# Building the expert gates: three bf16 parts against one fp32 product per token, with the scaling on ScalarE

## The chip, the cores and the metric

The kernel runs on one core of a Trainium2 chip, as one launch. The metric is the device time of that launch in microseconds (us). Five engines work side by side and meet only at semaphores: TensorE (PE, matrix products; PEld is its weight load), VectorE (DVE), ScalarE (ACT), GpSimd (POOL) and SyncE (SP), which here issues most of the DMAs.

## The reference, cut to what matters

Two trunk layers of a hybrid model are applied to 128 context ("prompt") tokens and 256 latent ("sample") tokens of width 1024. The change lies in the last part of each layer, a product-key expert mixer. Each token picks 16 experts for each of 8 heads, so 128 of 128 x 128 = 16384 experts, each with a gate from a softmax; an expert's number is i1 x 128 + i2.

```
e_idx = take_along_axis(cand_i, pos)          # 128 experts per token
gate  = softmax(top_s)                        # 8 heads x 16
a     = gelu(einsum('tkd,td->tk', peer_u[e_idx], x)) * gate
out   = einsum('tk,tkd->td', a, peer_v[e_idx])
```

## The kernel before, in words

The 128 prompt tokens are handled sparsely. Their expert rows (u and v, 8 KB each pair) are gathered from HBM, one expert of every token at a time (128 "rows" m per layer): POOL issues the gather, DVE takes the dot product with u (`dot_row`, line 1519), ACT applies Gelu and multiplies with the gate (`coefficient(m)`, lines 972 and 974), and DVE adds coefficient times v (`add_row(m)`, line 1513). `prompt_row` is `add_row(m)` followed by `dot_row` for m+1.

The 256 sample tokens are handled densely. TensorE computes the scores of all 16384 experts, 128 experts ("a panel") at a time, for all 256 tokens (`scores_u`, lines 512 to 517; a panel is split into a high and a low part, `split_panel_hi` on ACT, line 382, `split_panel_lo` on DVE or POOL, line 387). Each score panel goes through Gelu on ACT (line 965) into `act_t`, is multiplied there by the gate of each (token, expert), which is zero for most, and is multiplied with the v panels (`outputs_v`, line 704).

The dense gate table is built on TensorE, in two chunks of 64 values of i1. For a batch of 8 tokens, and for each token t of it, the gates are the product of two small matrices over that token's 128 choices: one-hot rows of i2 (128 x 128, tile `hot2`) and one-hot rows of i1 times the gate (128 x 64, tile `hot1`). The gate is fp32; it is cut into three bf16 parts (`gate_t`), so that each token takes three accumulating bf16 products (line 696). There are 32 batches per chunk.

Order of work in a layer around the change: first 64 score panels (with the routing of the tokens on DVE beside them). Then the **gating stage**, one batch and one score panel by turns, 32 times: on PE `scores_u`, then `build_gates(0, ...)`. Then a stage of scores and v panels ("mixed"). Then the **plain stage**, 32 times `outputs_v` followed by `build_gates(1, ...)`, with one prompt row per batch. Then the other v panels alone.

The order on each engine is the program's order. In the gating stage DVE does for batch w: `one_hots(w)`, `gate_acts(w-1)` (line 1584, the product's result times `act_t`), in every fourth batch (u = 0) a `prompt_row`, and in odd batches a `split_panel_lo`; ACT does `split_panel_hi` for two panels ahead and Gelu, with a `coefficient` first in every fourth batch; POOL does the `split_panel_lo` of even batches. In the plain stage DVE does `one_hots(w)`, `gate_acts(w-1)`, `prompt_row(w)`, and ACT only one `coefficient` per batch. `one_hots(w)` waits until the product of batch w-2 is done (two buffers); the product of batch w waits for `hot1`, `hot2` and for `gate_acts(w-2)`.

Of `one_hots`, four instructions per batch on DVE: `eq1` and `hot2` by comparing (line 1561), and two multiplications of `eq1` with the three gate parts into `hot1` (line 1569). The four tokens of a side lie interleaved in these tiles.

Of the kernel before, what the change touches and what calls it, by code (L numbers as in the profile page):

```python
# [27 lines left out]
BF16 = mybir.dt.bfloat16  # L28
U32 = mybir.dt.uint32
ALU = mybir.AluOpType  # L30
ACT = mybir.ActivationFunctionType
# [3 lines left out]
P = 128  # L35
# [17 lines left out]
HK = PH * TOPK  # L53
# [14 lines left out]
SLOTS = 4  # L68
# [15 lines left out]
TD = TS  # L84
DENSE = TD // P
CHUNKS = 2
CHUNK = NK // CHUNKS
BATCH = 8
SIDE = 4
NB = TD // BATCH  # L90
PARTS = 3
HALF = NB
SEATS = CHUNK + HALF
EARLY_G, HALF_G = CHUNK // SLOTS, HALF // SLOTS
# [3 lines left out]
RING = SLOTS  # L98
# [4 lines left out]
PLAIN_ROWS = MIXED_ROWS + HALF  # L103
LAST_ROWS = PLAIN_ROWS + HALF
# [15 lines left out]
def build(nc, panels, mod_panels, rows, x_in, c_in, vecs, g_final, k_cache, v_cache, bias_in, mask_in, dft_in,  # L120
# [4 lines left out]
    def place(name, where, cols, dt=F32):  # L125

        size = 2 if dt == BF16 else 4
        return nc.alloc_sbuf_tensor_at(name, [P, cols], dt, offset=where), where + size * cols


    raw, o = place("raw", base, SLOTS * D)
    split_hi, o = place("split_hi", o, 2 * D, F32R)
    split_lo, o = place("split_lo", o, 2 * D, F32R)
    h_hi_at = o
    h_hi, o = place("h_hi", o, KT * T, F32R)
    h_lo_at = o
    h_lo, o = place("h_lo", o, KT * T, F32R)
    x, o = place("x", o, KT * T)
    ident, o = place("ident", o, P)
    iota, o = place("iota", o, P)  # L140
    ones, o = place("ones", o, P)
    mask, o = place("mask", o, GRID_W)
    vec, o = place("vec", o, DEPTH * VEC)
    modv, o = place("modv", o, N_MOD * KT * 2)
    gain, o = place("gain", o, 2 * KT * 2)
    gfin, o = place("gfin", o, KT)
    softm, o = place("softm", o, 2 * 16)
# [4 lines left out]
    qkvf, o = place("qkvf", arena, 4 * KT * T)  # L152
    q, k, v, f = (qkvf[:, i * KT * T:(i + 1) * KT * T] for i in range(4))
    gate01, o = place("gate01", o, 2 * KT * T)
# [3 lines left out]
    conv, o = place("conv", o, KT * PAD)  # L158
    u_hi, o = place("u_hi", o, KT * T, F32R)
    u_lo, o = place("u_lo", o, KT * T, F32R)  # L160
    bias, o = place("bias", o, 2 * 2 * TS)
    kc_at = o
    kc, o = place("kc", o, HEADS * CTX)
    vc, o = place("vc", o, HEADS * DH)
    prob_at = o
    prob, o = place("prob", o, 2 * SCORES)
    prob_t, o = place("prob_t", o, 2 * SCORES)
    dft, o = place("dft", o, DFT)
    silu_c, mixer_end = place("silu_c", o, 2 * D)

    cc_s, o = place("cc_s", prob_at, 2 * T)
    ccx, o = place("ccx", o, 2 * PAD)
    cb_s, o = place("cb_s", o, 2 * T)
# [4 lines left out]
    f_hi, o = place("f_hi", arena, KT * T, F32R)  # L178
    f_lo, o = place("f_lo", o, KT * T, F32R)
    fy, _ = place("fy", o, 2 * TT * 512)  # L180

    sq, o = place("sq", arena + 4 * TT * D, KT * T)
    hf, o = place("hf", o, KT * T)
    ms, o = place("ms", o, T)
    rstd, _ = place("rstd", o, T)

    act_t, o = place("act_t", arena, SEATS * TD)
    late_seats = arena + 4 * CHUNK * TD
    act_end = o
    rowbuf, o = place("rowbuf", o, RING * ROW)  # L190
    htmp, _ = place("htmp", o - 4 * ROW, D)
    eq, eq_end = place("eq", o, 2 * HK * TOPK, BF16)
    hot2, o = place("hot2", o, 2 * BATCH * P, BF16)
    eq1, o = place("eq1", o, 2 * BATCH * CHUNK, BF16)
    hot1, o = place("hot1", o, 2 * BATCH * PARTS * CHUNK, BF16)
    assert eq_end <= o
    route_t, o = place("route_t", o, 2 * TD, BF16)
    gate_t, o = place("gate_t", o, PARTS * TD, BF16)
    gate_f, o = place("gate_f", o, TD)
    rest, o = place("rest", o, TD)  # L200
    index, o = place("index", o, SIDE * P, BF16)
    dots, o = place("dots", o, HK)
    dots_g, o = place("dots_g", o, HK)
    coef, o = place("coef", o, HK)
    gate0_r, o = place("gate0_r", o, HK)
    row_at, o = place("row_at", o, HK, U32)
    zeros, o = place("zeros", o, 2 * TD, BF16)
# [9 lines left out]
    sc2, o = place("sc2", o, TT * NK)  # L217
# [133 lines left out]
    def col(t, n, width=T):  # L351
        return t[:, n * width:(n + 1) * width]
# [147 lines left out]
    def _(pe):  # L500
# [44 lines left out]
        with pe.Fori(0, DEPTH) as l:  # L545
# [139 lines left out]
            def build_gates(chunk, turn, u):  # L685

                batch = (l * CHUNKS + chunk) * NB + turn * SLOTS + u
                pe.wait_ge(acts_gated, batch + 1)
                pe.wait_ge(hot2_ready, batch + 1)
                pe.wait_ge(hot1_ready[u % 2], (l * CHUNKS + chunk) * (NB // 2) + turn * 2 + u // 2 + 1)  # L690
                for t in range(BATCH):
                    seat_of = lambda h: h.rearrange("p (g j t) -> p g t j", g=BATCH // SIDE, t=SIDE)[:, t // SIDE, t % SIDE, :]
                    w = seat_of(col(hot2, u % 2, BATCH * P))
                    parts = col(hot1, u % 2, BATCH * PARTS * CHUNK)
                    for c in range(PARTS):
                        last = mm(col(bank[2 + u % 2], t, CHUNK), w, seat_of(col(parts, c, BATCH * CHUNK)), start=(c == 0),  # L696
                                  stop=(c == PARTS - 1))
                last.then_inc(gate_mm, 1)

            def outputs_v(act_at, g, s, last=False):  # L700
# [67 lines left out]
    def _(act):  # L768
# [42 lines left out]
        with act.Fori(0, DEPTH) as l:  # L811
# [182 lines left out]
            for t in range(DENSE):  # L994
                act.wait_ge(route_tr, l * DENSE + t + 1)
                copy(route_t[:, :].rearrange("p (j t) -> p j t", j=2)[:, :, t * P:(t + 1) * P],
                     bank[4 + t][:, 0:2 * P].rearrange("p (j t) -> p j t", j=2))
                copy(col(gate_t, t, P), col(bank[4 + t], 2, P))
                copy(col(gate_f, t, P), col(bank[4 + t], 2, P)).then_inc(route_stored, 1)
            for i in range(EARLY_G - 2, EARLY_G):  # L1000
                early(i, shared=True)

            def gating_turn(i, last=False):
                for u in range(SLOTS):
                    n = i + (FIRST["peer"] + EARLY_G)
                    if u == 0:
                        coefficient(i + EARLY_ROWS)
                    split_panel_hi(l, *ahead(n, u), at=u_seat(l, 0, u - 2) if last and u >= 2 else None)
                    gelu(n, u, CHUNK + i * SLOTS + u)
# [15 lines left out]
                mixed_turn(i)  # L1025
            mixed_turn(HALF_G - 1, last=True)
            act.wait_ge(gelu_ready, (l + 1) * NK)
            with act.Fori(PLAIN_ROWS // RING, HK // RING) as i:
                for b in range(RING):
                    coefficient(i * RING + b)  # L1030

# [108 lines left out]
    def _(dve):  # L1140
# [80 lines left out]
            dve.wait_ge(mod_loaded[s % 2], (n + 1) * 16)  # L1221
            modulation(V, col(mod_raw, s % 2, D), col(waste, s % 2, D), block, mod_used[s % 2])

        LAYER_STEPS = 347
        with dve.Fori(0, DEPTH) as l:
            layer = order.enter(l, 0, LAYER_STEPS)
            add_bias(l, SHIFT1 * KT, 2 * KT)
# [312 lines left out]
                shared(i)  # L1540
            carry(dve)
            dve.wait_ge(route_stored, (l + 1) * DENSE)
            g1, g2, g3 = [col(gate_t, c, TD) for c in range(PARTS)]
            order.step(V.tensor_tensor(rest[:, :], gate_f[:, :], g1, ALU.subtract))
            order.step(V.tensor_copy(g2, rest[:, :]))
            order.step(V.tensor_tensor(g3, rest[:, :], g2, ALU.subtract))

            carry(dve)
            for i in range(EARLY_G - 2, EARLY_G):
                shared(i)  # L1550
# [1 line left out]
            def one_hots(chunk, turn, u):  # L1552

                batch = (l * CHUNKS + chunk) * NB + turn * SLOTS + u
                dve.wait_ge(gate_mm, batch + 1)
                sides = BATCH // SIDE
                tokens = (turn * SLOTS + u) * BATCH
                for out, w, row, c0, done in ((eq1, CHUNK, 0, chunk * CHUNK, eq_ready),
                                              (hot2, P, 1, 0, hot2_ready)):
                    shape = [P, sides, w, SIDE]  # L1560
                    V.tensor_tensor(col(out, u % 2, BATCH * w).rearrange("p (g j t) -> p g j t", g=sides, t=SIDE),
                                    index[:, c0 * SIDE:(c0 + w) * SIDE].rearrange("p (j t) -> p j t", t=SIDE)
                                    .unsqueeze(1).broadcast_to(shape),
                                    route_t[:, bass.ds(tokens + row * TD, BATCH)].rearrange("p (g t) -> p g t", t=SIDE)
                                    .unsqueeze(2).broadcast_to(shape), ALU.is_equal).then_inc(done, 1)
                dve.wait_ge(eq_ready, batch + 1)
                shape = [P, PARTS, CHUNK, SIDE]
                for g in range(sides):
                    last = V.tensor_tensor(  # L1569
                        col(hot1, u % 2, BATCH * PARTS * CHUNK).rearrange("p (c g j t) -> p c g j t", c=PARTS, g=sides,  # L1570
                                                                          t=SIDE)[:, :, g, :, :],
                        col(col(eq1, u % 2, BATCH * CHUNK), g, SIDE * CHUNK).rearrange("p (j t) -> p j t", t=SIDE)
                        .unsqueeze(1).broadcast_to(shape),
                        gate_t[:, :].rearrange("p (c t) -> p c t", c=PARTS)[:, :, bass.ds(tokens + g * SIDE, SIDE)]
                        .unsqueeze(2).broadcast_to(shape), ALU.mult)
                last.then_inc(hot1_ready[u % 2], 1)

            def gate_acts(chunk, turn, u):

# [180 lines left out]
```

## Time and profile before

| | us |
|---|---|
| median of 3 runs (lowest, highest) | 3404.49 (3401.98, 3405.86) |
| the profiled execution | 3406.33 |
| its span, first to last instruction | 3404.2 |
| PE busy | 3172.6 (93%) |
| DVE busy | 2262.4 (66%) |
| ACT busy | 993.6 (29%) |
| POOL busy | 1269.1 (37%) |
| gate products (line 696), PE busy, 3072 of them | 211.8 |
| idle of PE ahead of them | 45.0 |

PE is busy nearly all the time, but busy time of matmuls overlaps in the records, and the chain of work that ended last is PE for 86% of the span. The costs of an edit are read from the stretch in which it stands: the timeline shows there which instruction each engine started when, and what ended its wait. Granted clock 1.00 is the 2.4 GHz level of TensorE, and a mean below it is a mixture with its 1.2 GHz level.

### The profile page before, as it was taken

How to read it: one execution, taken by the hardware profiler on the slowest of the kernel's cores; microseconds unless marked ns; L12 is line 12 of the kernel's file. 1: busy time of each engine (PE TensorE's matmuls, PEld its weight loads, DVE VectorE, ACT ScalarE, POOL GpSimd, SP SyncE). 2: the span in 40 equal slices, each digit the busy share in tenths (PEclk: the TensorE clock that was granted, in tenths of full speed). 3: DMA queues.
4: the chain of work that ended last, by engine and by line, in shares of the span. 5: the costliest groups of instructions: out<-in, count | busy, mean ns of one | idle time of the engine just before them, and what ended most of it. 6: DMA issues, size and time to landing. Idle time of an engine off the chain costs nothing.

```text
span 3404.2 us, 61704 instructions
## 1 busy us (share of the span) xinstructions
PE 3172.6 (93%) x20514; PEld 2951.9 (87%) x20516; DVE 2262.4 (66%) x4081; ACT 993.6 (29%) x1823; POOL 1269.1 (37%) x855
## 2 busy tenths in 40 slices
PE   4999989899988999999989998998989899999998
PEld 3999879798888999987879998797889889999877
DVE  7398543489688557976345884336887875599662
ACT  3334422345422221011033343233544222311110
POOL 0333213258843333333114332133787332333430
PEclk7999999899989999999989999998999999999999
DMA  5377513234754898899635773132357459898993
GB/s 226 135 247 253 167 56 107 82 120 164 257 178 158 297 330 328 316 368 418 256 132 170 250 252 118 43 130 81 136 191 266 157 179 334 323 323 315 401 417 135
DMA packets 172882, 750.46 MB, mean 220 GB/s; under 512 B 19056, under 2 KB 23536, under 8 KB 138992
## 3 DMA queue, kind: packets, MB, share of 16 engines
q1 hardware_dynamic: 128304, 467.98, 39.7%
q0 software_dynamic: 36864, 268.45, 20.7%
q10 hardware_dynamic: 7616, 12.85, 1.1%
q8 instruction: 46, 0.75, 0.1%
q14 instruction: 52, 0.43, 0.0%
HBM read 745.53 MB, written 3.67 MB: 220 GB/s over the span
## 4 chain that ended last, share of the span: by engine, by line
PE 86%; DVE 4%; issue 3%; ACT 2%; POOL 2%; DMA 1%; ACTq 0%; DVEq 0%; POOLq 0%; SPq 0%
PE bank L704 26%; PE bank L517 17%; PE bank L512 17%; PE bank L513 16%; PE bank L696 6%; POOL split_lo L387 1%; PE bank L607 1%; ACT split_hi L382 1%; PE bank L628 1%; DMA raw<-panels 1%; DVE h_lo L1177 1%; DVE hot L1569 1%; PE bank L661 1%; PE bank L533 0%; PE bank L502 0%
## 5 line engine op out<-in xcount | busy, mean ns | idle before, releaser
L387 POOL TENSOR_TENSOR split_lo<-raw,split_hi 128x1024 fp32r<-128x1024 f32 x290 | 768.4, 2652 | 1229.6 <-ACT split_hi L382 1228.7
L512 PE MATMUL bank<-h_hi,split_hi 128*128 128x256 f32 (+1 forms) x3712 | 1100.7, 317 | 67.8 <-DVE h_lo L1177 63.0
L513 PE MATMUL bank<-h_lo,split_hi 128*128 128x256 f32 (+1 forms) x3712 | 1073.8, 310 | 0.0
L704 PE MATMUL bank<-act_t,raw 128*128 (+1 forms) x4096 | 929.5, 382 | 7.1 <-DVE act_t L1584 2.6
L382 ACT ACTIVATE split_hi<-raw 128x1024 fp32r<-128x1024 f32 x512 | 542.9, 1061 | 1324.6 <-PE bank L517 1052.8
L704 PEld LDWEIGHTS bank<-act_t,raw 128*128 128x128 f32 x4096 | 763.6, 190 | 133.6 <-issue 37.7
L512 PEld LDWEIGHTS bank<-h_hi,split_hi 128*128 128x128 f32 x3712 | 717.3, 193 | 88.4 <-DVE h_lo L1177 79.5
L513 PEld LDWEIGHTS bank<-h_lo,split_hi 128*128 128x128 f32 x3712 | 718.0, 193 | 1.6
L517 PE MATMUL bank<-h_hi,split_lo 128*128 128x256 f32 (+1 forms) x3712 | 619.0, 309 | 25.7 <-POOL split_lo L387 25.7
L387 DVE TENSOR_TENSOR split_lo<-raw,split_hi 128x1024 fp32r<-128x1024 f32 x222 | 277.9, 1252 | 503.2 <-ACT split_hi L382 502.6
L517 PEld LDWEIGHTS bank<-h_hi,split_lo 128*128 128x128 f32 x3712 | 563.5, 193 | 29.7 <-POOL split_lo L387 29.7
L1513 DVE SCALAR_TENSOR_TENSOR acc<-rowbuf,coef,acc 128x1024 f32<-128x1024 f32 x256 | 330.9, 1293 | 136.2 <-ACT coef L974 135.7
L1519 DVE SCALAR_TENSOR_TENSOR rowbuf<-rowbuf,h 128x1024 f32<-128x1024 f32 x256 | 349.1, 1364 | 27.3 <-DMA rowbuf<-rows,row_ring 26.7
L1102 POOL COPY row_ring<-row_at 128x1 uint32 (+1 forms) x256 | 175.4, 685 | 502.2 <-DVE acc L1513 502.1
L1105 POOL DMA_INDIRECT rowbuf<-rows,row_ring x256 | 275.2, 1075 | 220.8 <-POOL row_ring L1102 213.6
L696 PE MATMUL bank<-hot,hot 128*128 128x64 bf16 x3072 | 211.8, 242 | 45.0 <-DVE hot L1569 45.0
L696 PEld LDWEIGHTS bank<-hot,hot 128*128 128x128 bf16 x3072 | 196.3, 118 | 59.6 <-issue 37.5
L972 ACT ACTIVATE dots_g<-dots (+1 forms) x256 | 51.4, 201 | 594.0 <-DVE rowbuf L1519 593.2
L403 DVE SCALAR_TENSOR_TENSOR waste<-mod_raw,silu_c 128x1024 bf16<-128x1024 f32 x96 | 175.0, 1823 | 47.5 <-DMA mod_raw<-mod_panels 47.5
L1569 DVE TENSOR_TENSOR hot<-eq,gate_t 128x768 bf16<-128x768 bf16 x256 | 136.2, 571 | 0.0
L403 DVE SCALAR_TENSOR_TENSOR mod_raw<-mod_raw,silu_c 128x1024 f32<-128x1024 f32 x96 | 121.0, 1260 | 0.0
L965 ACT ACTIVATE act_t<-bank 128x256 f32 (+1 forms) x256 | 93.9, 367 | 24.0 <-PE bank L704 23.8
(173 smaller groups left out, 2429.9 us busy)
## 6 DMA issues: line engine op xcount, KB each, us to landing
raw<-panels SPq DMA_DIRECT2D x768, 512.0 KB, 4.1
mod_raw<-mod_panels SPq DMA_DIRECT2D x96, 512.0 KB, 4.3
raw<-mod_panels SPq DMA_DIRECT2D x16, 512.0 KB, 5.2
bias<-bias_in ACTq DMA_DIRECT2D x16, 256.0 KB, 2.7
rowbuf<-rows,row_ring POOLq DMA_INDIRECT x256, 8.4
silu_c<-c_in SPq DMA_DIRECT2D x3, 1024.0 KB, 6.2
dft<-dft_in ACTq DMA_DIRECT2D x2, 1152.0 KB, 5.9
subk<-sub_keys ACTq DMA_DIRECT2D x2, 1024.0 KB, 6.2
```

Of the source, the lines that this page charges most:

```text
L382: nc.scalar.activation(col(split_hi, s % 2, D), col(raw, slot, D), ACT.Copy).then_inc(hi_ready[s], 1)
L387: eng.tensor_tensor(col(split_lo, s % 2, D), col(raw, slot, D), col(split_hi, s % 2, D).bitcast(F32), ALU.subtract).then_inc(lo_ready[s], 1)
L403: last = eng.scalar_tensor_tensor(waste if m == 0 else panel, panel, 1.0, col(silu_c, m, D), ALU.mult, ALU.mult, accum_out=modv[:, bass.ds ...
L512: mm(out, w_hi, rhs(rhs_hi, kk), start=(kk == 0), stop=False)
L513: mm(out, w_hi, rhs(rhs_lo, kk), start=False, stop=False)
L517: last = mm(out, w_lo, rhs(rhs_hi, kk), start=False, stop=(kk == KT - 1))
L696: last = mm(col(bank[2 + u % 2], t, CHUNK), w, seat_of(col(parts, c, BATCH * CHUNK)), start=(c == 0), stop=(c == PARTS - 1))
L704: m = mm(col(bank[4 + kk // 2], kk % 2, TD), col(col(raw, s, D), kk, P), act_t[:, bass.ds(act_at * TD, TD)], start=False, stop=last and kk ...
L1102: pool.tensor_copy(row_ring[:, b:b + 1], row_at[:, bass.ds(m, 1)]).then_inc(row_copied, 1)
L1105: pool.indirect_dma_start(col(rowbuf, b, ROW), None, rows, bass.IndirectOffsetOnAxis(ap=row_ring[:, b:b + 1], axis=0)).then_inc(rows_loade ...
L1513: V.scalar_tensor_tensor(acc0, half, coef[:, bass.ds(m, 1)], acc0, ALU.mult, ALU.add).then_inc(acc_done, 1)
L1519: V.scalar_tensor_tensor(half, half, 1.0, h0, ALU.mult, ALU.mult, accum_out=dots[:, bass.ds(i * RING + b, 1)]).then_inc(dot_ready, 1)
```

## The change

The three bf16 parts go. `hot2` and `hot1` become fp32 and lie token by token; PE does one plain fp32 product per token (8 per batch for 24). DVE makes `eq1` as before, and `hot2` with fp32 output by comparing `iota`; the two multiplications into `hot1` leave DVE. In their place ACT scales, for each of the 8 tokens of a batch, a 128 x 64 slice of `eq1` by that token's gate column (`gate_hots`). In ACT's order `gate_hots` of a batch stands ahead of the `coefficient`, the split and the Gelu of that batch. The three DVE instructions that cut the gate into parts, and two ACT copies per layer, go.

```diff
-    hot2, o = place("hot2", o, 2 * BATCH * P, BF16)
+    hot2, o = place("hot2", o, 2 * BATCH * P)
-    hot1, o = place("hot1", o, 2 * BATCH * PARTS * CHUNK, BF16)
+    hot1, o = place("hot1", o, 2 * BATCH * CHUNK)
...
                 for t in range(BATCH):
-                    for c in range(PARTS):
-                        last = mm(col(bank[2 + u % 2], t, CHUNK), w, seat_of(col(parts, c, BATCH * CHUNK)), start=(c == 0),
-                                  stop=(c == PARTS - 1))
+                    last = mm(col(bank[2 + u % 2], t, CHUNK), col(col(hot2, u % 2, BATCH * P), t, P),
+                              col(col(hot1, u % 2, BATCH * CHUNK), t, CHUNK), start=True, stop=True)
...
+            def gate_hots(chunk, turn, u):
+                act.wait_ge(eq_ready, (l * CHUNKS + chunk) * NB + turn * SLOTS + u + 1)
+                for t in range(BATCH):
+                    hot = col(eq1, u % 2, BATCH * CHUNK).rearrange("p (g j t) -> p g t j", g=BATCH // SIDE, t=SIDE)
+                    last = nc.scalar.activation(col(col(hot1, u % 2, BATCH * CHUNK), t, CHUNK),
+                                                hot[:, t // SIDE, t % SIDE, :], ACT.Copy,
+                                                scale=gate_f[:, bass.ds((turn * SLOTS + u) * BATCH + t, 1)])
+                last.then_inc(hot1_ready[u % 2], 1)
...
             def gating_turn(i, last=False):
                 for u in range(SLOTS):
                     n = i + (FIRST["peer"] + EARLY_G)
+                    gate_hots(0, i, u)
                     if u == 0:
                         coefficient(i + EARLY_ROWS)
...
-            with act.Fori(PLAIN_ROWS // RING, HK // RING) as i:
+            with act.Fori(0, HALF_G) as i:
+                for u in range(SLOTS):
+                    gate_hots(1, i, u)
+                    coefficient(PLAIN_ROWS + i * SLOTS + u)
+            with act.Fori(LAST_ROWS // RING, HK // RING) as i:
...
-            g1, g2, g3 = [col(gate_t, c, TD) for c in range(PARTS)]
-            order.step(V.tensor_tensor(rest[:, :], gate_f[:, :], g1, ALU.subtract))
-            order.step(V.tensor_copy(g2, rest[:, :]))
-            order.step(V.tensor_tensor(g3, rest[:, :], g2, ALU.subtract))
...
+                V.tensor_tensor(col(eq1, u % 2, BATCH * CHUNK).rearrange("p (g j t) -> p g j t", g=sides, t=SIDE),
...
+                                ALU.is_equal).then_inc(eq_ready, 1)
+                shape = [P, BATCH, P]
+                V.tensor_tensor(col(hot2, u % 2, BATCH * P).rearrange("p (t j) -> p t j", t=BATCH),
+                                iota[:, :].unsqueeze(1).broadcast_to(shape),
+                                route_t[:, bass.ds(tokens + TD, BATCH)].unsqueeze(2).broadcast_to(shape),
+                                ALU.is_equal).then_inc(hot2_ready, 1)
```

## Rows read from the trace of the kernel before

**Rows 1.** Stages' windows: busy us (count) of PE, PEld, DVE, ACT, POOL; clock, DMA.

```profile
948.00:1116.00 168.00, 149.77 (x1537) 146.67 (x1539) 132.68 (x200) 44.56 (x79) 59.81 (x33) 0.94 0.46 156
1318.00:1479.00 161.00, 159.69 (x1280) 143.90 (x1279) 157.72 (x257) 16.10 (x65) 62.87 (x65) 1.00 0.89 319
```

**Rows 2.** Timeline, plain stage, one batch, three engines: start, duration, instruction [idle before].

```profile
1403.61 1.22 DVE L1519 SCALAR_TENSOR_TENSOR rowbuf<-rowbuf,h 128x1024 f32<-128x1024 f32 x1
1404.75 0.42 DVE L1561 TENSOR_TENSOR eq<-index,route_t 128x512 bf16<-128x512 bf16 x1
1404.95 0.20 ACT L972 ACTIVATE dots_g<-dots  x1 [4.33 <-DVE rowbuf L1519]
1405.00 1.66 PE L696 MATMUL bank<-hot,hot 128*128 128x64 bf16 x24
...
1405.29 0.30 ACT L974 ACTIVATE coef<-dots_g,gate_r  x1
...
1406.48 3.69 PE L704 MATMUL bank<-act_t,raw 128*128 x16
1406.80 0.69 DVE L1584 TENSOR_TENSOR act_t<-act_t,bank 128x512 f32 x1
1407.41 1.28 DVE L1513 SCALAR_TENSOR_TENSOR acc<-rowbuf,coef,acc 128x1024 f32<-128x1024 f32 x1
1408.61 1.22 DVE L1519 SCALAR_TENSOR_TENSOR rowbuf<-rowbuf,h 128x1024 f32<-128x1024 f32 x1
...
1409.75 0.42 DVE L1561 TENSOR_TENSOR eq<-index,route_t 128x512 bf16<-128x512 bf16 x1
```

**Rows 3.** Timeline of PE, gating stage: product starts through one turn of four batches.

```profile
1041.12 1.66 PE L696 MATMUL bank<-hot,hot 128*128 128x64 bf16 x24 [2.52 <-DVE hot L1569]
1045.55 1.66 PE L696 MATMUL bank<-hot,hot 128*128 128x64 bf16 x24
...
1054.48 1.66 PE L696 MATMUL bank<-hot,hot 128*128 128x64 bf16 x24
1061.57 1.65 PE L696 MATMUL bank<-hot,hot 128*128 128x64 bf16 x24 [2.51 <-DVE hot L1569]
```

**Rows 4.** Timeline of ACT, DVE and POOL, gating stage, around one such wait.

```profile
1008.62 1.07 ACT L382 ACTIVATE split_hi<-raw 128x1024 fp32r<-128x1024 f32 x1 [3.16 <-PE bank L517]
...
1009.72 1.23 DVE L387 TENSOR_TENSOR split_lo<-raw,split_hi 128x1024 fp32r<-128x1024 f32 x1 [3.40 <-ACT split_hi L382]
...
1010.86 0.42 DVE L1561 TENSOR_TENSOR eq<-index,route_t 128x512 bf16<-128x512 bf16 x1
...
1014.19 3.81 POOL L387 TENSOR_TENSOR split_lo<-raw,split_hi 128x1024 fp32r<-128x1024 f32 x1 [6.51 <-ACT split_hi L382]
1014.53 1.22 DVE L1519 SCALAR_TENSOR_TENSOR rowbuf<-rowbuf,h 128x1024 f32<-128x1024 f32 x1
...
1015.67 2.60 DVE L1561 TENSOR_TENSOR eq<-index,route_t 128x512 bf16<-128x512 bf16 x1
```

**Rows 5.** POOL's splits by their line: count, shortest/median/longest ns.

```profile
L387 POOL TENSOR_TENSOR split_lo<-raw,split_hi x290: 2346/2411/4419, 49.2 to 2780.3; 128x1024 fp32r<-128x1024 f32 x145
```

**Rows 6.** ACT groups by form, 53 to 61 us: count, busy us, mean ns.

```profile
L798 ACT ACTIVATE h_hi<-hf,modv 128x256 fp32r<-128x256 f32 x6 | 3.0, 492 | 0.0
L798 ACT ACTIVATE h_hi<-hf,modv 128x128 fp32r<-128x128 f32 x7 | 2.8, 399 | 5.5 <-DVE hf L1167 5.5
```

**Rows 7.** Timeline of ACT, four of these in a row, sizes alternating.

```profile
53.36 1.49 ACT L798 ACTIVATE h_hi<-hf,modv 128x128 fp32r<-128x128 f32 x4 [2.66 <-DVE hf L1167]
```

**Rows 8.** Timeline of PE: six records of plain fp32 products, 128 columns, and the next.

```profile
658.23 0.83 PE L661 MATMUL bank<-subk,pq 128*128 x6
658.82 0.42 PE L512 MATMUL bank<-h_hi,split_hi 128*128 128x384 f32 x1
```

**Rows 9.** Timeline of DVE, first batch of the gating stage.

```profile
945.27 3.28 DVE L1569 TENSOR_TENSOR hot<-eq,gate_t 128x768 bf16<-128x768 bf16 x2
```

**Rows 10.** DVE group by form, layer's end: two instances, idle before, releaser.

```profile
L1640 DVE SCALAR_TENSOR_TENSOR x<-bank,modv,x 128x128 f32<-128x128 f32 x16 | 5.5, 344 | 114.9 <-PE bank L502 114.9
```

More of the change, by code:

```diff
@@ L90 @@
 NB = TD // BATCH
-PARTS = 3
 HALF = NB
@@ L192, in build @@
     eq, eq_end = place("eq", o, 2 * HK * TOPK, BF16)
-    hot2, o = place("hot2", o, 2 * BATCH * P, BF16)
+    hot2, o = place("hot2", o, 2 * BATCH * P)
     eq1, o = place("eq1", o, 2 * BATCH * CHUNK, BF16)
-    hot1, o = place("hot1", o, 2 * BATCH * PARTS * CHUNK, BF16)
+    hot1, o = place("hot1", o, 2 * BATCH * CHUNK)
     assert eq_end <= o
     route_t, o = place("route_t", o, 2 * TD, BF16)
-    gate_t, o = place("gate_t", o, PARTS * TD, BF16)
     gate_f, o = place("gate_f", o, TD)
-    rest, o = place("rest", o, TD)
     index, o = place("index", o, SIDE * P, BF16)
@@ L691, in build_gates @@
                 for t in range(BATCH):
-                    seat_of = lambda h: h.rearrange("p (g j t) -> p g t j", g=BATCH // SIDE, t=SIDE)[:, t // SIDE, t % SIDE, :]
-                    w = seat_of(col(hot2, u % 2, BATCH * P))
-                    parts = col(hot1, u % 2, BATCH * PARTS * CHUNK)
-                    for c in range(PARTS):
-                        last = mm(col(bank[2 + u % 2], t, CHUNK), w, seat_of(col(parts, c, BATCH * CHUNK)), start=(c == 0),
-                                  stop=(c == PARTS - 1))
+                    last = mm(col(bank[2 + u % 2], t, CHUNK), col(col(hot2, u % 2, BATCH * P), t, P),
+                              col(col(hot1, u % 2, BATCH * CHUNK), t, CHUNK), start=True, stop=True)
                 last.then_inc(gate_mm, 1)
@@ L997, in _ @@
                      bank[4 + t][:, 0:2 * P].rearrange("p (j t) -> p j t", j=2))
-                copy(col(gate_t, t, P), col(bank[4 + t], 2, P))
                 copy(col(gate_f, t, P), col(bank[4 + t], 2, P)).then_inc(route_stored, 1)
@@ L1222, in mod_panel @@
             modulation(V, col(mod_raw, s % 2, D), col(waste, s % 2, D), block, mod_used[s % 2])
-        LAYER_STEPS = 347
+        LAYER_STEPS = 344
         with dve.Fori(0, DEPTH) as l:
@@ L1557, in one_hots @@
                 tokens = (turn * SLOTS + u) * BATCH
[L1558 to L1575, printed above, removed]
@@ L1576, in one_hots @@
-                last.then_inc(hot1_ready[u % 2], 1)
+                shape = [P, sides, CHUNK, SIDE]
+                V.tensor_tensor(col(eq1, u % 2, BATCH * CHUNK).rearrange("p (g j t) -> p g j t", g=sides, t=SIDE),
+                                index[:, chunk * CHUNK * SIDE:(chunk + 1) * CHUNK * SIDE]
+                                .rearrange("p (j t) -> p j t", t=SIDE).unsqueeze(1).broadcast_to(shape),
+                                route_t[:, bass.ds(tokens, BATCH)].rearrange("p (g t) -> p g t", t=SIDE)
+                                .unsqueeze(2).broadcast_to(shape), ALU.is_equal).then_inc(eq_ready, 1)
```

## The prediction

> **What bounds the kernel now.** I read the busy windows by stage first, then the timeline of one period in each stage that the change touches, then the rows of single operations. In the plain stage PE is busy 159.7 of 161 us and DVE 157.7; ACT only 16.1. In the gating stage PE is busy 149.8 of 168 us, ACT 44.6, at a mean granted clock of 0.94 [rows 1]. So on paper ACT is nearly free and both stages are PE's.
>
> The timelines say it more exactly. In the plain stage a batch takes 5.00 us, from one `eq` to the next. PE spends 1.48 us of it from the first gate product to the first v product, and 3.52 us on the v panel; nothing waits [rows 2]. That the 24 bf16 products are done in 1.48 us gives 62 ns for each, start to start. In the gating stage the products of a turn of four batches start at 0, 4.43, (8.9), 13.36 and 20.45 us: three intervals of 4.43 to 4.5, which is PE's own work (2.95 of scores and 1.48 of gates), and one of 7.09, with a wait of 2.5 us for DVE's one-hots [rows 3]. The wait's cause is on DVE: after the prompt row of u = 0, `eq` takes 2.60 us in place of 0.42. It ends 0.27 us after a `split_lo` of POOL that had been waiting in its turn for DVE's dot (3.81 us for a median of 2.41) [rows 4, 5]. The two engines hold each other up here, and POOL goes first. The Trainium skill says so in "SBUF — State Buffer", section "Who interferes with whom": a VectorE instruction with two SBUF inputs and a GpSimd one that reads SBUF lock each other out for a whole instruction, whoever starts first. The trace agrees (2.60 against 0.42); what it makes possible is rival two.
>
> At a layer's end DVE waits 114.9 us, twice 57, for PE: prompt rows that come late by less than 57 us in a layer cost nothing of themselves [rows 10].
>
> **The change, part by part.**
>
> *ACT's scaling.* 128 batches in all get 8 scalings each, of 128 x 64. The trace has no such instruction. Activations with a per-partition operand take 399 ns for 128 columns and 492 for 256 [rows 6], and 300 for one column with the gate as scale [rows 2]; 64 columns lie between, at 348. Four in a row, two of each size, take 1.49 us where their durations sum to 1.78, so neighbours overlap by 0.10 [rows 6, 7]. Step s: 0.25 us, nearest to these rows; bounds 0.20 (0.30 less the overlap) and 0.40 (the 128-column row without overlap). Eight occupy ACT for 2.0 us, and from the first start to the last end they take 2.1.
>
> *The plain stage.* Here lies the main cost, and no busy share shows it. `gate_hots` of batch w stands in ACT's order ahead of `coefficient` m of that batch, and waits for `eq` of w. DVE's `add_row` m waits for that coefficient, then comes the dot, and only then the next `eq`. So a closed ring arises between the engines, one turn per batch, of which before only the coefficient was a part, and had time: ACT computed it while DVE made its one-hots. The ring: `eq` 0.42; to ACT 0.12 (as from the dot's end, 1404.83, to line 972, 1404.95); eight steps 2.0; coefficient 0.64 (1404.95 to 1405.59); back 0.12; from the start of the add to the next `eq` 2.34 [all rows 2]. Sum 5.64 us against 5.00: 0.64 x 32 x 2 = +41 us. With the bounds of s, 5.24 and 6.84: +15 and +118.
>
> What lies beside the ring: `hot2`, now 1024 fp32 results, 1.23 us by the nearest row, a DVE split of that size [rows 4], and `gate_acts` 0.69, so 1.9 us in the 2.9 that DVE waits for ACT. The multiplications that leave DVE were beside work already, so their going gives nothing here. Bounds of `hot2`: 0.42 (`eq`, half the elements, bf16) and 2.60 (a blocked one); with the upper 3.3 us would not fit in 2.9, and the ring would grow by 0.4, +26 us over both layers.
>
> *The fp32 product.* Eight products per batch; plain fp32 appears as two records per product (as at line 704, 16 records for 8), so 16 records for 24. Lower bound 62 ns each as now [rows 2], 0.98 us; upper bound the plain fp32 product with 128 columns, twice the moving width, 111 ns ((0.83 - 0.275) / 5, the last record's own 275 ns left out) or 98 by the start of the next line [rows 8]: 1.78 or 1.57. I take 1.7, near the rows of the same kind, against 1.48 now. PE needs then 3.52 + 1.7 = 5.2 us per batch in the plain stage, still inside the ring's 5.64, so its price does not decide there; at the upper bound 5.3 neither. The Trainium skill, "TensorE: Matmul & The Clock Gate", sections "LDWEIGHTS (loading the stationary operand)" and "Weight-path perf modes", speaks against the change: fp32 weights get no fast load, and 128 columns take P / 1.2, 107 ns. By that the batch would cost an estimated 1.71 us, by the lower bound from the rows 0.98; the sum would differ by some 12 us, all in the gating stage's one interval that PE still sets.
>
> *The gating stage.* I follow one turn from the end E of a batch's scalings, with the same steps. u = 0 to 1: coefficient (now behind the scalings) done at E + 0.54, add at 0.66, dot ends 3.08; `eq` ends 2.52 after that, as now (1015.75 to 1018.27, POOL's split between) at 5.60; 0.12 + 2.1 more: 7.82, for 7.09. 1 to 2: ACT's split comes only after the scalings, to E + 0.97, DVE's split and `eq` (0.03 + 1.14 + 0.42) to 2.56, scalings to 4.78, for 4.43. 2 to 3: PE's own 2.95 + 1.7 = 4.65. 3 to 0: from PE's scores 0.1 to ACT, split 1.07, 0.03, 1.14, 0.42, 0.12, 2.1, and 0.12 to PE: 5.10. Sum 22.35 against 20.45: +1.9 us, 8 turns, 2 layers: +30 [rows 3, 4]. Bounds: s = 0.20 with a product of 0.98 gives 20.43, nothing; s = 0.40 gives 25.95, +88.
>
> *First batch and small things.* The pair of multiplications took 3.28 us at the stage's start, and `hot2` stood between them and `eq`; scalings need 2.2 from `eq`. That gives back 1.1 to 1.7, take 1.5, per layer: -3 us [rows 9]. The three DVE steps on the gate parts and the two ACT copies lie beside score panels: nothing.
>
> *Clock.* Eight turns of 20.45 are 163.6 us of a stage of 168 at 0.94, so the low level costs about 4 us a layer now [rows 1, 3]. The long wait grows from 2.5 to about 3.2 us and two short ones join it. I double the cost, +8; bounds 0 and +24.
>
> Sum: 41 + 30 - 3 + 8 = +76. Made against the profiled execution's 3406.33, that is 3482; the median of the runs is 1.84 lower, so 3480.
>
> **The rivals.**
>
> One: the scalings don't overlap, since each reads its own scale column (s = 0.348, 2.78 us for eight). Ring 6.42, +91; turn 24.4, +63; with -3 and +8: +159, 3563. For it: no two such instructions with a scale operand stand in a row in the trace. Against it: those of rows 7 have an operand per partition and overlap.
>
> Two: POOL loses its race in the gating stage. The prompt row there now starts later against POOL's split; if the split runs between other DVE work, `eq` takes 0.42, the interval is 5.64 in place of 7.82, the turn 35 us less over both layers, and the clock stays high. Then 41 - 5 - 3 = +33: 3437. Against it: by my times POOL still comes 1.4 us before the dot ends. For it: the order of the starts decides, and both start anew.
>
> Three, faster: the ring stays hidden, and PE gains. At 62 ns a record PE's batch shrinks by 0.50: 64 times in the plain stage, 48 in the three PE-bound intervals of the gating stage: -56, with the -3 for the first batches 3345. It decides only where the ring is shorter than PE's 4.50, so eight scalings under 0.86 us, 0.11 each. Against it: 300 ns for one column.
>
> Four, no effect: something that I count in series lies beside PE work in both stages, 3404.
>
> **How the numbers follow.** My forecast 0.58, rival one 0.16, two 0.14, three 0.08, four 0.04. The range reaches down to 3418, the low ends of all terms (+15, 0, -3, 0) and rival two within it, and up to 3560, about the middle of rival one; what is left out is three, four and half of one, 0.2. The forecast's own range is 3445 to 3520. Within 0.2% (6.8 us) is about what a measurement cannot tell from no change; slower 0.88, same 0.04, faster 0.08.
>
> **What would show it.** Right: in the plain stage a period of 5.5 to 5.8 us, ACT busy about half of it, line 1513 on DVE waiting for the coefficient in every batch, PE idle about 0.4 us per batch ahead of the gate products, for ACT. In the gating stage turns of about 22.4 us with 7.8 in one interval, `eq` still 2.6 us there. The gate products at 100 to 111 ns a record. Wrong: a plain period of 5.0 to 5.3 with PE never idle (then PE decides, and the fp32 price is what counts), scalings more than 0.3 us apart (rival one), or `eq` never blocked (rival two).

## The result and the profile after

The changed kernel takes 3494.28 us (median of 4 runs, 3489.41 to 3494.44) against 3403.43 (4 runs): a ratio of 1.0263, 95% interval [1.0245, 1.0281]. It is slower by 90.9 us, where 76 were forecast. The profiled execution is the shortest of the four, 3489.41, with a span of 3487.6 us, 83.4 more than before; the accounts by stage below are of these spans. Two later executions, one of fill_before (3870.8 us) and one of the kernel before beside it (12437.58 us), were slow and are left out of the comparisons.

Busy time by stage, the changed kernel, first layer (length, then busy us and count of PE, PEld, DVE, ACT, POOL; clock, DMA share, GB/s):

```profile
943.00:1132.00 189.00, 164.72 (x1276) 161.88 (x1277) 122.96 (x135) 107.45 (x331) 60.70 (x34) 0.93 0.41 142
1335.00:1517.00 182.00, 174.03 (x1018) 150.40 (x1017) 143.35 (x192) 77.80 (x320) 74.56 (x64) 1.00 0.78 279
```

Against [rows 1] the gating stage is 21 us longer and the plain stage 21. ACT is still far from full in either (57% and 43%), DVE is less busy than before, and PE has gaps in the plain stage that it did not have. No engine's busy share explains either stage.

One period of the plain stage, same kernel, the lines that answer to [rows 2] (start, duration, instruction, idle before):

```profile
1424.39 0.42 DVE L1561 TENSOR_TENSOR eq<-index,route_t 128x512 bf16<-128x512 bf16 x1
1424.73 1.22 DVE L1567 TENSOR_TENSOR hot<-iota,route_t 128x1024 f32<-128x1024 f32 x1
1424.94 2.05 ACT L1000 ACTIVATE hot<-eq,gate_f 128x64 f32<-128x64 bf16 x8 [3.10 <-DVE eq L1561]
1425.87 0.68 DVE L1578 TENSOR_TENSOR act_t<-act_t,bank 128x512 f32 x1
1426.90 0.19 ACT L965 ACTIVATE dots_g<-dots  x1
1427.21 0.29 ACT L967 ACTIVATE coef<-dots_g,gate_r  x1
1427.73 1.28 DVE L1520 SCALAR_TENSOR_TENSOR acc<-rowbuf,coef,acc 128x1024 f32<-128x1024 f32 x1 [1.19 <-ACT coef L967]
1428.93 1.22 DVE L1526 SCALAR_TENSOR_TENSOR rowbuf<-rowbuf,h 128x1024 f32<-128x1024 f32 x1
1430.08 0.42 DVE L1561 TENSOR_TENSOR eq<-index,route_t 128x512 bf16<-128x512 bf16 x1
```

The reader can walk the ring in these lines: `eq`, eight scalings, coefficient, add, dot, the next `eq` 5.69 us after the last. ACT waits 3.10 us for DVE, and DVE 1.19 for ACT, in each turn of it. Each has time to spare; neither can use it.

The gating stage, starts of the gate products on PE, the lines that answer to [rows 3]:

```profile
1037.49 2.00 PE L689 MATMUL bank<-hot,hot 128*128 128x64 f32 x16 [0.33 <-ACT hot L1000]
1045.37 2.49 PE L689 MATMUL bank<-hot,hot 128*128 128x64 f32 x16 [2.96 <-ACT hot L1000]
1051.64 1.90 PE L689 MATMUL bank<-hot,hot 128*128 128x64 f32 x16
1056.30 1.90 PE L689 MATMUL bank<-hot,hot 128*128 128x64 f32 x16
1061.45 2.00 PE L689 MATMUL bank<-hot,hot 128*128 128x64 f32 x16 [0.33 <-ACT hot L1000]
```

The intervals are 7.88, 6.27, 4.66 and 5.15 us: a turn of 23.96 for 20.45. Around the long one, ACT, DVE and POOL, the lines that answer to [rows 4]:

```profile
1037.92 1.06 ACT L379 ACTIVATE split_hi<-raw 128x1024 fp32r<-128x1024 f32 x1
1038.08 1.28 DVE L1520 SCALAR_TENSOR_TENSOR acc<-rowbuf,coef,acc 128x1024 f32<-128x1024 f32 x1 [1.08 <-ACT coef L967]
1039.13 2.48 POOL L384 TENSOR_TENSOR split_lo<-raw,split_hi 128x1024 fp32r<-128x1024 f32 x1 [7.70 <-ACT split_hi L379]
1039.28 3.41 DVE L1526 SCALAR_TENSOR_TENSOR rowbuf<-rowbuf,h 128x1024 f32<-128x1024 f32 x1
1042.62 0.41 DVE L1561 TENSOR_TENSOR eq<-index,route_t 128x512 bf16<-128x512 bf16 x1
```

POOL's split now comes 0.15 us ahead of the dot, and the dot takes 3.41 us for 1.22. `eq` behind it is not held up any more (0.43 us at most from the first gate product on); the delay has moved one instruction forward.

### The profile page after: what moved, and what is told of

It reads as the page before. It is cut to its first block, busy times and chain, and to the rows that moved or that the text cites. A ratio compares the mean times of both kernels' runs of the same rounds, so it can differ in the third digit from the quotient of the medians.

```text
span 3487.6 us, 61388 instructions
## 1 busy us (share of the span) xinstructions
PE 3238.2 (93%) x19492; PEld 3003.9 (86%) x19492; DVE 2202.5 (63%) x3819; ACT 1243.8 (36%) x2843; POOL 1303.6 (37%) x855
## 4 chain that ended last, share of the span: by engine, by line
PE 72%; issue 10%; ACT 7%; DVE 6%; POOL 2%; ACTq 1%; DVEq 1%; DMA 1%; POOLq 0%; SPq 0%
PE bank L697 20%; PE bank L514 15%; PE bank L509 15%; PE bank L510 15%; ACT hot L1000 4%; PE bank L689 2%; POOL split_lo L384 1%; PE bank L604 1%; ACT split_hi L379 1%; DVE eq L1561 1%; DVE rowbuf L1526 1%; PE bank L625 1%; ACT coef L967 1%; ACTq L1000 1%; DVE h_lo L1184 1%
## 5 line engine op out<-in xcount | busy, mean ns | idle before, releaser
L384 POOL TENSOR_TENSOR split_lo<-raw,split_hi 128x1024 fp32r<-128x1024 f32 x290 | 746.5, 2576 | 1273.9 <-ACT split_hi L379 1273.0
L1109 POOL COPY row_ring<-row_at 128x1 uint32 (+1 forms) x256 | 205.9, 804 | 506.1 <-DVE acc L1520 506.0
L1526 DVE SCALAR_TENSOR_TENSOR rowbuf<-rowbuf,h 128x1024 f32<-128x1024 f32 x256 | 369.1, 1442 | 32.6 <-DMA rowbuf<-rows,row_ring 32.1
L1112 POOL DMA_INDIRECT rowbuf<-rows,row_ring x256 | 301.1, 1176 | 220.8 <-POOL row_ring L1109 213.6
L1000 ACT ACTIVATE hot<-eq,gate_f 128x64 f32<-128x64 bf16 x1024 | 262.2, 339 | 307.1 <-DVE eq L1561 307.1
L689 PEld LDWEIGHTS bank<-hot,hot 128*128 128x128 f32 x2048 | 248.2, 198 | 95.7 <-DVE act_t L1578 65.8
L689 PE MATMUL bank<-hot,hot 128*128 128x64 f32 x2048 | 261.6, 283 | 65.2 <-ACT hot L1000 62.2
L1567 DVE TENSOR_TENSOR hot<-iota,route_t 128x1024 f32<-128x1024 f32 x128 | 155.8, 1217 | 0.0
```

Of the source, the lines that this page charges most:

```text
L384: eng.tensor_tensor(col(split_lo, s % 2, D), col(raw, slot, D), col(split_hi, s % 2, D).bitcast(F32), ALU.subtract).then_inc(lo_ready[s], 1)
L689: last = mm(col(bank[2 + u % 2], t, CHUNK), col(col(hot2, u % 2, BATCH * P), t, P), col(col(hot1, u % 2, BATCH * CHUNK), t, CHUNK), start= ...
L1000: last = nc.scalar.activation(col(col(hot1, u % 2, BATCH * CHUNK), t, CHUNK), hot[:, t // SIDE, t % SIDE, :], ACT.Copy, scale=gate_f[:, ba ...
L1112: pool.indirect_dma_start(col(rowbuf, b, ROW), None, rows, bass.IndirectOffsetOnAxis(ap=row_ring[:, b:b + 1], axis=0)).then_inc(rows_loade ...
L1526: V.scalar_tensor_tensor(half, half, 1.0, h0, ALU.mult, ALU.mult, accum_out=dots[:, bass.ds(i * RING + b, 1)]).then_inc(dot_ready, 1)
```

## The experiments

All are compared with the changed kernel's 3494.28 unless said otherwise; the kernel before ran beside each group, with medians between 3402.8 and 3404.6. The changed kernel itself ran only for the result.

**coef_plain: the ring cut in the plain stage.**

```diff
-                    gate_hots(1, i, u)
                     coefficient(PLAIN_ROWS + i * SLOTS + u)
+                    gate_hots(1, i, u)
```

> The changed kernel with one swap: in the plain stage ScalarE computes the row's coefficient ahead of the batch's eight scalings, not behind them. Theory ring (DVE's eq, ACT's scalings, coefficient, DVE's add and dot, next eq form one closed chain of 5.69 us): the coefficient leaves the chain, the period falls to PE's own 3.52 + 1.81 = 5.33 us, 64 times 0.36 is -23 us, about 3471. Rival price (the fp32 products set the period, the wait for ACT is incidental): period and time stay, 5.69 us and 3494.

Measured 3466.02 (3464.42 to 3467.47), -28.3 us; 1.0182 of before, [1.0165, 1.0199]. Its plain stage in the timeline, ACT and PE of one period:

```profile
1420.10 0.20 ACT L965 ACTIVATE dots_g<-dots  x1 [2.59 <-DVE rowbuf L1526]
1420.14 1.89 PE L689 MATMUL bank<-hot,hot 128*128 128x64 f32 x16
1420.43 0.30 ACT L967 ACTIVATE coef<-dots_g,gate_r  x1
1420.67 2.05 ACT L1000 ACTIVATE hot<-eq,gate_f 128x64 f32<-128x64 bf16 x8
1421.88 3.67 PE L697 MATMUL bank<-act_t,raw 128*128 x16
1425.38 1.89 PE L689 MATMUL bank<-hot,hot 128*128 128x64 f32 x16
```

The same instructions in another order on ACT, and the period is 5.24 us, with PE never idle; 0.45 x 64 is 28.8. So the ring cost this, and below it lies PE's own time with the fp32 products: 1.74 us per batch from the first gate product to the first v product, for 1.48 before. The expectation had reckoned 1.81, hence its smaller gain.

**coef_gate: the same swap in the gating stage.**

```diff
-                    gate_hots(0, i, u)
                     if u == 0:
                         coefficient(i + EARLY_ROWS)
+                    gate_hots(0, i, u)
```

> The changed kernel with the same swap in the gating stage alone: the coefficient of every fourth batch stands ahead of that batch's scalings, as before the change. Theory ring: the prompt row starts 1.1 us earlier, the long interval falls from 7.88 to about 6.7 us, PE's wait in it from 2.96 to about 1.8; if the low clock behind it comes from that wait, the next interval falls too, from 6.27 to about 4.8: 16 turns, -19 us without and -43 with the clock. Rival (POOL's split and DVE hold each other up whatever the order, so the row ends as late): no change, 3494.

Measured 3465.50 (3462.94 to 3473.27), -28.8 us. The products' starts in one turn:

```profile
1042.61 1.97 PE L689 MATMUL bank<-hot,hot 128*128 128x64 f32 x16 [1.77 <-ACT hot L1000]
1047.33 1.99 PE L689 MATMUL bank<-hot,hot 128*128 128x64 f32 x16
1052.08 1.90 PE L689 MATMUL bank<-hot,hot 128*128 128x64 f32 x16
1057.24 2.00 PE L689 MATMUL bank<-hot,hot 128*128 128x64 f32 x16 [0.35 <-ACT hot L1000]
```

The long interval is 6.69, its wait 1.77, as expected. The interval behind it is 4.72 in this turn, but 6.2 or 7.8 in 6 of 14 turns: the clock term went half way, and the time lies between the two ends given. (The first turn of each layer, with its own wait, is left out of these counts.)

**coef_both: both swaps.**

> The changed kernel with the coefficient ahead of the scalings in both stages. Theory ring: the two gains of the single swaps are in different stages and add up, -28 and -29: 3437, which leaves +33 over the kernel before: 0.24 x 64 = 15 in the plain stage for the fp32 product, the rest in the gating stage. Rival: one is worth nothing once the other is done, 3465.

Measured 3436.64 (3432.47 to 3438.99), -57.6: the sum of the two is -57.1. The two costs are apart from each other.

**one_bf16: a single bf16 product.**

```diff
-    hot2, o = place("hot2", o, 2 * BATCH * P)
+    hot2, o = place("hot2", o, 2 * BATCH * P, BF16)
-    hot1, o = place("hot1", o, 2 * BATCH * CHUNK)
+    hot1, o = place("hot1", o, 2 * BATCH * CHUNK, BF16)
```

> The changed kernel with both one-hot tiles in bf16, so one bf16 product per token: the gate is rounded to bf16, two of its three parts are left out. PE's gate work falls from 1.81 to about 0.5 us per batch, ACT's and DVE's instructions stay. Theory ring: the plain period stays at 5.6 to 5.7 us, PE only idles 1.3 us more; in the gating stage only the interval that PE sets (4.66 us) and the one at low clock fall, -1.2 and about -1 us, 16 turns: about -35 us in all, 3459. Rival price: 1.3 us less in nearly each of 128 batches, period 4.4 us, -130 to -165 us, below 3365.

Measured 3450.74 (3449.51 to 3451.75), -43.5. The plain stage on PE:

```profile
1424.62 0.39 PE L689 MATMUL bank<-hot,hot 128*128 128x64 bf16 x8 [1.82 <-ACT hot L1000]
1425.30 5.40 PE L697 MATMUL bank<-act_t,raw 128*128 x16 [0.28 <-issue]
1430.54 0.40 PE L689 MATMUL bank<-hot,hot 128*128 128x64 bf16 x8
1430.77 3.70 PE L697 MATMUL bank<-act_t,raw 128*128 x16
1435.98 0.39 PE L689 MATMUL bank<-hot,hot 128*128 128x64 bf16 x8 [1.51 <-ACT hot L1000]
```

From 1317.0 to 1492.7 us 31 periods take 5.67 each, as in the changed kernel (1336.5 to 1512.4: 5.67). PE's gate work falls from 1.74 to some 0.4 us per batch, and the stage is no shorter: PE's price does not set it. In three of four batches PE now waits 1.4 to 1.9 us ahead of the gate products; in about every fourth, as in the first one shown, the v panel takes 5.40 us for 3.70, at a mean granted clock of 0.71 from 1424.6 to 1430.5 us, and that fills the time of the wait. The gain comes in the gating stage: the interval that PE sets falls from 4.66 to between 3.3 and 3.6, some 18 us over both layers, and the one behind the long wait from between 6.2 and 7.8 to between 4.7 and 5.7, some 19. The clock in that interval is no higher (0.50 to 0.70), but PE has less to do in it. The rival's 3365 is out by 86 us.

**fp32_dve: the fp32 product without ACT in the chain.**

```diff
-                    gate_hots(0, i, u)
-                    gate_hots(1, i, u)
...
+                dve.wait_ge(eq_ready, batch + 1)
+                for g in range(sides):
+                    shape = [P, SIDE, CHUNK]
+                    last = V.tensor_tensor(
+                        col(col(hot1, u % 2, BATCH * CHUNK), g, SIDE * CHUNK).rearrange("p (t j) -> p t j", t=SIDE),
+                        col(col(eq1, u % 2, BATCH * CHUNK), g, SIDE * CHUNK).rearrange("p (j t) -> p t j", t=SIDE),
+                        gate_f[:, bass.ds(tokens + g * SIDE, SIDE)].unsqueeze(2).broadcast_to(shape), ALU.mult)
+                last.then_inc(hot1_ready[u % 2], 1)
```

> The changed kernel with the scaling moved back to DVE (two multiplications per batch, fp32 result), ACT's scalings gone, the fp32 product kept. This is the fp32 product alone, without ACT in the chain. Theory ring: the plain period falls to PE's 5.33 us, +21 us over the kernel before; in the gating stage three PE-bound intervals of 4.43 become 4.76 and the long one stays about 7.1 to 7.4: +16 to +20; in all about 3445. Rival price: as the changed kernel, 3480 to 3494, since the product is unchanged.

Measured 3451.75 (3448.86 to 3451.95), 1.0137 of before, [1.012, 1.0154]: +47, for about +41 expected. The plain period is 5.24, PE's, as in coef_plain:

```profile
1423.23 1.89 PE L689 MATMUL bank<-hot,hot 128*128 128x64 f32 x16
1424.96 3.67 PE L697 MATMUL bank<-act_t,raw 128*128 x16
1428.47 1.89 PE L689 MATMUL bank<-hot,hot 128*128 128x64 f32 x16
```

0.24 x 64 gives 15. A turn of the gating stage has 7.37, 4.66 and 4.77 us and, behind the wait, 4.72 to 7.87 us, at least 1.07 more than before, 17 in 16 turns. The rest of the 47 is mostly the interval behind the wait, which is over 6 us in 10 of 14 turns, for 5 of 14 before that were longer than 4.5 (5.1 to 6.6).

**fill_after and fill_before: PE kept busy through the wait.**

```diff
                     scores_u(i + (FIRST["peer"] + EARLY_G), u)
+                    if u == 1:
+                        for _ in range(11):
+                            mm(bank[6][:, :], zeros[:, 0:P], zeros[:, :], start=True, stop=True)
                     build_gates(0, i, u)
```

> The changed kernel with 11 bf16 products of zeros on PE in each turn of the gating stage, between the scores and the gate product of u = 1, where PE waits 2.96 us; they go to a bank that nothing reads. Theory clock (PE idles in the long interval, the granted clock falls to 1.2 GHz, and the interval behind it takes 6.27 to 7.8 us in place of 4.72): with PE busy through the wait the clock stays, the intervals behind fall to about 4.75, sum over 16 turns about -22 us, 3472. Rival (those intervals are long because hot1 comes late again, not for the clock): they stay at 6.27, and the products of zeros cost nothing or a little, 3494 to 3500.

> The kernel before with 9 such products of zeros in the same place, where PE waits 2.5 us. In its trace only six of the sixteen intervals behind the wait are long (5.1 to 6.6 us against 4.42). Theory clock: these become 4.42, -9 to -11 us, 3394, a little faster than the kernel before. Rival: no change, or slower by the products' time.

fill_after: 3472.68 (3471.63 to 3473.52), -21.6. The interval behind the wait by windows, the changed kernel first, then fill_after:

```profile
1045.40:1051.60 6.20, 6.20 (x40) 6.20 (x41) 4.76 (x6) 3.09 (x10) 0.00 (x0) 0.72 0.72 254
1069.30:1075.60 6.30, 6.28 (x41) 6.30 (x41) 4.76 (x6) 3.15 (x10) 0.00 (x0) 0.73 0.72 251
```

```profile
1044.90:1049.60 4.70, 4.70 (x40) 4.67 (x41) 3.82 (x6) 3.09 (x10) 0.00 (x0) 1.00 0.90 312
1067.40:1072.10 4.70, 4.70 (x40) 4.67 (x41) 3.82 (x6) 3.09 (x10) 0.00 (x0) 1.00 0.91 311
```

The same 40 products of PE take 6.2 us at a mean clock of 0.72 (part of the time at 1.2 GHz) and 4.7 at 1.00. The products of zeros do no useful work and change no wait of `hot1` (the long interval is still 7.89); they only keep PE active. So this interval is the clock's. fill_before gives 3399.0 against 3403.2, a ratio of 0.9988, [0.9979, 0.9998]: the intervals behind the wait are now all 4.40 to 4.43, but only about 4.2 us come back, half of what was expected. The expectation counted six long intervals; there are five (6.57, 5.64, 5.13, 6.51 and 5.60 us), 7.4 us over 4.42 in all. And in the first turn of each layer, where PE had gone to the low clock already, the zeros themselves lengthen the interval (8.2 us for 6.2 to 6.5), which takes back some 3.7 us. In fill_after's first turns they take back some 3.

**row_before and row_u2: the prompt row elsewhere in the turn.** Kernel before, DVE:

```diff
-                if u == 0:
+                if u == 1:
                     m = EARLY_ROWS + n
                     prompt_row(m // RING, m % RING)
```

> The kernel before with the gating stage's prompt row moved on DVE from behind gate_acts of u = 0 to behind that of u = 1. Theory (the long interval of 7.09 us comes from the prompt row and POOL's split, which stand ahead of the one-hots of u = 1): these one-hots are then ready in time, and the row falls into DVE's idle time behind them; the turn falls from 20.45 towards PE's 17.7, up to -40 us, 3365 to 3380. Rival: DVE's work and POOL's splits exclude each other anywhere in the turn, so the wait only moves to the next batch: 3400 to 3410.

> The kernel before with the gating stage's prompt row behind gate_acts of u = 2, a batch whose split is POOL's, as that of u = 0 is; the row at u = 1, a batch whose split is DVE's, gave 3378. Theory POOL (the wait of 2.5 us comes from the row meeting POOL's split of the same batch): the long interval only moves to u = 3, turn about 20.4, time 3395 to 3408. Rival (any place but u = 0 is better, since the one-hots of u = 1 were the late ones): 3375 to 3385.

row_before: 3378.05 (3377.65 to 3379.43), 0.9924 of before, [0.9908, 0.994]: it beats both kernels. The products' starts in one turn:

```profile
1040.47 1.67 PE L696 MATMUL bank<-hot,hot 128*128 128x64 bf16 x24
1044.91 1.67 PE L696 MATMUL bank<-hot,hot 128*128 128x64 bf16 x24
1049.35 1.67 PE L696 MATMUL bank<-hot,hot 128*128 128x64 bf16 x24
1054.77 1.66 PE L696 MATMUL bank<-hot,hot 128*128 128x64 bf16 x24 [0.83 <-DVE hot L1569]
1059.48 0.72 PE L696 MATMUL bank<-hot,hot 128*128 128x64 bf16 x9
```

A turn takes 19.0 us; the wait of 2.5 has become 0.83, one batch later. DVE and POOL still collide, as these lines of the same kernel show, but not ahead of the one-hots of u = 1: the add of the row waits, and these one-hots stand ahead of it. (A second collision in the turn, on `eq` of u = 3, 2.56 us at 1055.23, delays PE by 0.2 us at most.)

```profile
1046.17 1.02 DVE L1569 TENSOR_TENSOR hot<-eq,gate_t 128x768 bf16<-128x768 bf16 x2
1046.33 3.14 POOL L387 TENSOR_TENSOR split_lo<-raw,split_hi 128x1024 fp32r<-128x1024 f32 x1 [7.82 <-ACT split_hi L382]
1047.70 2.85 DVE L1513 SCALAR_TENSOR_TENSOR acc<-rowbuf,coef,acc 128x1024 f32<-128x1024 f32 x1
```

At u = 2 the wait only moves: 3408.92 (3405.66 to 3413.26), 1.0015 of before, [1.0006, 1.0025], just above the 3395 to 3408 of this theory and far from its rival's 3375 to 3385. Its `eq` of u = 3 takes 2.60 us, and PE waits the same 2.51 as in [rows 3]:

```profile
1041.55 3.94 POOL L387 TENSOR_TENSOR split_lo<-raw,split_hi 128x1024 fp32r<-128x1024 f32 x1 [4.27 <-ACT split_hi L382]
1043.17 2.60 DVE L1561 TENSOR_TENSOR eq<-index,route_t 128x512 bf16<-128x512 bf16 x1
1047.46 1.64 PE L696 MATMUL bank<-hot,hot 128*128 128x64 bf16 x24 [2.51 <-DVE hot L1569]
```

**row_coef: the changed kernel with both swaps and the row at u = 1.**

> The changed kernel with the coefficient ahead of the scalings in both stages and the prompt row of the gating stage at u = 1. Theory (the change's cost is its ring, its fp32 product and the row's place, and no more): against 3437 with the coefficient moved, the long interval of 6.69 falls to about 5.7 and the low-clock intervals behind it to 4.7: -16 to -25, about 3415. It would still lose to the kernel before by the 0.24 us per batch that PE pays in the plain stage (15 us). Rival: ACT, with splits, Gelu and scalings in one order, then sets the gating stage, and little changes: 3430 or more.

Measured 3404.93 (3403.21 to 3409.42): 1.0002 of before, [0.9993, 1.0012], and 10 us below the 3415 expected. Its turns are 4.76, 5.24, 4.76 and 5.15 us with waits of 0.42 and 0.33. So nearly all of the 91 us goes by reordering alone, some 25 of it by the row's new place, which the kernel before gains as well. Beside row_before, which has the same place for the row, the change still costs 27: 15 from 0.24 x 64 in the plain stage, 15 from turns of 19.9 for 19.0; the other stretches differ by a few us either way.

**tok_hot2: which operand's step costs a bf16 product.** In one_bf16 eight products take 0.39 us with the last one's 0.19: below 30 ns each, where they were 62 before.

```diff
-                    w = seat_of(col(hot2, u % 2, BATCH * P))
+                    w = col(col(hot2, u % 2, BATCH * P), t, P)
```

(with `hot2` made as in the changed kernel, in bf16).

> The kernel before with hot2 alone token by token (still bf16, compared from iota by DVE as in the changed kernel); hot1 stays interleaved, 24 bf16 products per batch. In one_bf16, where both tiles lie token by token, eight products start 24 to 30 ns apart; before, with both interleaved, 62. Theory weights (the step of eight bytes in the stationary operand is what costs): products about 25 to 30 ns apart, 0.7 us per batch. Rival moving (the step in the moving operand costs): 62 as before. Time: DVE's hot2 takes 1.22 in place of 0.68 us, and DVE was busy 157.7 of 161 us in the plain stage, so DVE sets a period of about 5.4 us there whichever holds: +25 us, and +10 in the gating stage: 3430 to 3445.

Measured 3454.53 (3450.88 to 3456.34), 1.015 of before, slower than expected. The plain period is 5.33 us, near the 5.4 expected; the gating stage, from its first gate product to its last, grew to 174.5 us in both layers from 162.7 and 161.6, some 25 us for the 10 expected. In the plain stage:

```profile
1404.40 1.60 PE L696 MATMUL bank<-hot,hot 128*128 128x64 bf16 x24 [0.15 <-DVE hot L1573]
1405.82 3.69 PE L704 MATMUL bank<-act_t,raw 128*128 x16
```

24 products in 1.42 us are 59 ns each: laying the stationary operand token by token changes next to nothing. The products start some 60 ns apart from the second of a batch on, here and in the kernel before, so it is not that 24 stand in a row. What is left between these products and those of one_bf16 is the moving operand's step of four elements, and that three products accumulate here; the two were not tried apart.

## Why the prediction was right

*The ring* was the main term and held: 5.69 us for 5.64, 43.4 us over both layers (the stretches from the first mixed product to the layer's last update grew by 21.8 and 21.6) for 41. The step s is 0.244 us ((2.05 - 0.34) / 7, one scaling being 0.34) for 0.25 between [rows 6] and [rows 7]; rival one, scalings without overlap, is out. PE's idle time was forecast as 0.4 us per batch. The rows list 0.27 in every second batch only, by modelled ends of the products; the period of 5.68 less the 5.24 that PE needs without waits (coef_plain) is 0.44. coef_plain and one_bf16 show the ring from both sides.

*The fp32 product*: 1.74 us against 1.7, and as forecast it set no period as long as the ring stood. The prediction's estimate from the Trainium skill, "TensorE: Matmul & The Clock Gate", section "LDWEIGHTS (loading the stationary operand)" (107 ns per fp32 load, 1.71 us), agrees with this trace, 109 ns a record. The lower bound of 62 ns, taken from the bf16 rows, says little of fp32 records: one_bf16's products, with another layout of the operands, start 29 ns apart. The sum did not use it; the low end of the gating stage and rival three's time did.

*The gating stage's turn*: 7.82, 4.78, 4.65 and 5.10 were forecast, 22.35 in all; 7.88, 4.72 (at the full clock, fill_after), 4.66 and 5.15 came, 22.4. So this term, +30, held as well, but not by the path named for the long interval: the collision with POOL hit the dot (3.41 us), and `eq` took 0.41. The forecast's sign of it, `eq` still at 2.6, was wrong, and `eq` never blocked had been named as the sign of rival two. That the size held all the same is luck in part: the delay is one POOL split whichever instruction waits, 2.18 us on `eq` before and 2.19 on the dot now. The prediction's own times had POOL start 1.4 us ahead of the end of a dot that takes 1.22, so ahead of its start; it did not ask whether the dot would then be held. Rival two, a gain from the race, did not come.

*The clock* is the term that was mis-sized: +8 was forecast. In the changed kernel the interval behind the wait is at low clock in all 14 turns counted, 6.25 to 7.80 us for 4.72, some 24 us in all, of which fill_after gives back 21.6; before it was 5 of 14, 7.4 us, of which fill_before gives back 4.2. So the cost tripled, where the forecast had it double: by the intervals and by the two fills alike the change's part in it is 17 us, 9 more than the forecast. Of the 83.4 us between the two profiled executions this is what the forecast of 76 mainly lacked, with the ring's 2; the 5.4 named below goes the other way. The medians differ by 90.9, since the execution profiled before was 2.9 us above its median and the one after 4.9 below; no trace shows these last 7.5.

*First batch*: PE's wait ahead of the first gate product fell from 4.95 us to 3.13 and 3.14, -3.6 for the -3 forecast. Another 5.4 us by which the stretches ahead of these two waits were shorter in this execution have no cause in the change that I can name; kernels with the same instructions up to there reach the first layer's first gate product up to 3.1 us apart (the changed one, coef_plain, fill_after) or 3.8 (the one before, fill_before, row_before, row_u2).

Rivals three and four are out: PE waits in the plain stage, and nothing was hidden.

## What to carry to other kernels

Before work is moved to an engine that seems free, draw the order of both engines through one period: if A waits for B's work and B for A's within one iteration, the sum of both is a floor on the period, whatever their busy shares. Where an instruction that feeds the ring's other half stands behind new work in its engine's order, put it ahead; here that swap gave 28 us in each stage. And look which instruction stands behind an exclusive collision of two engines: it can be cheaper to let another one wait, as row_before does, than to avoid it.

## What the runs showed of the hardware

- DVE and POOL held each other up in nearly every turn: `eq` took 2.60 us for 0.42 (14 of 16 turns before), the dot 3.41 for 1.22 (all 16 of the changed kernel), the add 2.85 for 1.28 (row_before). The Trainium skill, "SBUF — State Buffer", section "Who interferes with whom", says that two such instructions lock each other out for a whole instruction and that the order of issue decides; the durations agree. The recorded starts do not show the order: in [rows 4] POOL's split starts 0.34 us ahead of the dot, yet the dot runs through in 1.22 and the split takes 3.81; in the changed kernel it starts 0.15 us ahead, and the dot waits. What decides was not settled.
- PE's clock after a wait: low behind all 14 waits of 2.8 to 3.0 us (the changed kernel), 10 of 14 of 2.44 to 2.49 (fp32_dve), 5 of 14 of 2.5 (before), 6 of 14 of 1.76 to 1.80 (coef_gate); mean granted clock 0.52 to 0.73 in those intervals, 1.00 in the others. The length of the wait alone doesn't order these; what else decides was not settled.
- A bf16 product of 64 columns cost 62 ns with both operands interleaved by four tokens and 59 with only the moving one, three accumulating; it cost under 30 with neither interleaved, one per token. Whether the moving operand's layout or the accumulation makes the difference is open.
